# Lower experts' rows gathered and added on POOL during the last MoE blocks, and the last block's y added by a slot matrix on PE

## The chip, the cores and the metric

One core of one Trainium2 chip runs the whole program. The metric is the device time of one execution in microseconds (us), the median of three runs. Names of engines: PE (TensorE), DVE (VectorE), ACT (ScalarE), POOL (GpSimd), SP (SyncE, which issues loads).

## The reference, cut to what matters

A token mixer (not touched by the change) gives `x` for 544 tokens (512 of a prompt, 32 samples) of width 1024. Then:

```python
def grouped_moe(x, w_router, router_bias, w_gate, w_up, w_down):
    xt = x.reshape(B * T, D)
    probs = jax.nn.softmax(xt @ w_router + router_bias, axis=-1)      # 16 experts in 4 groups of 4
    grp_score = lax.top_k(grp, TOP_K)[0].sum(-1)
    g_idx = lax.top_k(grp_score, 1)[1][:, 0]                          # one group for each token
    top_w, top_i = lax.top_k(jnp.where(emask, probs, -1.0), TOP_K)    # two experts inside it
    top_w = top_w / jnp.sum(top_w, axis=-1, keepdims=True)
    for e in range(N_EXPERTS):
        h = jax.nn.silu(xt @ w_gate[e]) * (xt @ w_up[e])
        y = y + gates[:, e:e + 1] * (h @ w_down[e])

x = layer_norm(ALPHA * x + grouped_moe(x, ...), ln2_g, ln2_b)
```

All is f32. A token has two experts, both in one group of four consecutive experts.

## The kernel before, in words

The tokens are five tiles (four of 128 rows, one of 32). After the mixer and the first layer norm, x1 stands in `xr` and in DRAM by token (`x1_by_token`). DVE computes the routing and a slot for each of the 2 x 544 choices: expert e owns the 128 slots of block e, and up to eight overflow blocks take what doesn't fit (their count, `n_over`, is read at the end; with these inputs it is 0). `slot_f` and `slot_i` hold ten columns, five tiles for the first choice and five for the second, `gw` their gates.

Then 16 blocks follow, one expert each, in the order of their numbers. Each engine has its own written order, `step(bi, par)`, with semaphores between them. For block b:

* SP (`moe_loads`, L505 on) loads six chunks of weights of 1 MB each (gate in two, up in two, and down of block b-1 in two) into a ring of eight `raw` places, as soon as DVE has used the chunk eight before.
* ACT (`mhi`, L859) rounds a chunk to f32r, DVE (`mlo`, L1322) subtracts to get the low part: a 128x2048 tensor_tensor whose two inputs are both in SBUF. PE makes three products (hi hi, hi lo, lo hi) of each piece: `gate_up` (L1777) and `down` (L1789). There are three places for split chunks.
* POOL gathers the x1 rows of the next block by `ids` (`gather`, L629), and stores the y of two blocks before from `ysb[par]` to `y_by_slot` in DRAM (`store`, L646). y leaves PSUM in two halves, one by ACT (L882), one by DVE (`y_half`, L1339).
* PE transposes x (`x_turn`, L1767) and h (`h_turn`, L1799); ACT and DVE copy them to hi and lo (L864, L869, L1327, L1332). `hidden` (L1347) multiplies silu(gate) and up on DVE.

After block 15, POOL waits for both stores, reads the overflow count (L661), and issues ten indirect gathers (L672), two for each tile, into `y_a` and `y_b`, which lie where `raw` was. DVE makes eleven diagonal matrices (`diag`, L1411 and L1415): ALPHA, and the gates of each tile and choice. PE's `weigh` (L1865) forms, for each tile and each half of 512 columns, ALPHA x + g1 y_a + g2 y_b in PSUM, as three f32 products with a diagonal as weights; those with x for tiles 0 to 3 come before the gathers have landed. The fifth tile uses the banks of the first, so it waits for DVE to have read them (`s_fg`). Then DVE takes mean and variance (L1425, L1428), subtracts and scales (L1431), ACT takes the root (L945) and scales the tile (L949), POOL adds the bias (L677), SP stores. For the last tile DVE does scale and bias itself (L1438).

In front of block 0, DVE does `first_lo` for three chunks, then `overflow_table` (L1302 to L1308, 22 small linked operations), then `x_lo(0, 0)`, for which PE's first product waits. At the very start of the program POOL fills the overflow blocks of `y_by_slot` with zeros (L574), 8 blocks in one DMA.

## Time and profile before

| what | value |
|---|---|
| three runs | 698.58, 697.02, 699.57 us; median 698.58 |
| the run that was profiled | 699.09 us, its span 697.3 us |
| PE busy | 663.2 us (95%), 3847 instructions |
| DVE busy | 505.2 us (72%) |
| ACT busy | 344.4 us (49%) |
| POOL busy | 134.8 us (19%) |
| granted TensorE clock, mean | 0.976 |

The span is the time from the first to the last event of the profile; the run's own time is 1.8 us longer. The profile names a group of instructions by line, engine, operation, and `written tile<-read tiles`, and puts idle time before an instruction down to what ended it. Matmul records are pipelined, and an f32 product of 512 columns shows as two records.

### The profile page before, as it was taken

The page shows a single profiled execution, that of the slowest core. Times are in us where ns is not written, and L with a number is a line of the kernel's source. Part 1 is how long each engine was busy: PE and PEld are TensorE (multiplying, and loading weights), DVE is VectorE, ACT ScalarE, POOL GpSimd, SP SyncE. Part 2 cuts the span into 40 slices and gives each one's busy share as a digit, 9 for nine tenths or more (in the row PEclk, how much of TensorE's full clock was granted, in tenths as well). Part 3 has the DMA queues.
Part 4 walks back from the last instruction along what each step waited for, and adds up shares of the span by engine and source line. Part 5 has one row for each costly group of instructions (what it writes and reads, how often), then busy time and mean ns, then how long its engine had stood idle before and what let it go on. Part 6 is the DMA issues. An engine that isn't in the chain of part 4 may idle for free. (4 is left out here: it accounts for less than half of the span.)

```text
span 697.3 us, 9659 instructions
## 1 busy us (share of the span) xinstructions
PE 663.2 (95%) x3847; PEld 559.2 (80%) x3847; DVE 505.2 (72%) x579; ACT 344.4 (49%) x339; POOL 134.8 (19%) x81
## 2 busy tenths in 40 slices
PE   6999999988999999999979999999999999999786
PEld 5999899988997897577857888888888888888531
DVE  4226336798766384758684999999999999999626
ACT  4537412222226141111505777777777777777402
POOL 0001414422131220400020011111111111100055
PEclk9999999999999999999898999999999999999998
DMA  8951111211612105069346999999999999994164
GB/s 285 381 198 62 61 61 62 69 53 61 190 53 85 53 16 193 0 185 410 138 160 274 328 417 419 397 415 409 407 415 411 404 413 406 410 404 173 47 242 158
DMA packets 48689, 162.56 MB, mean 233 GB/s; under 512 B 4294, under 2 KB 23450, under 8 KB 36364
## 3 DMA queue, kind: packets, MB, share of 16 engines
q1 hardware_dynamic: 41756, 136.62, 51.4%
q0 software_dynamic: 6896, 25.43, 9.3%
q8 instruction: 25, 0.41, 0.2%
q14 instruction: 12, 0.10, 0.0%
HBM read 142.61 MB, written 19.44 MB: 232 GB/s over the span
## 5 line engine op out<-in xcount | busy, mean ns | idle before, releaser
L1322 DVE TENSOR_TENSOR RA<-FA,RA 128x2048 fp32r<-128x2048 f32 x93 | 212.9, 2290 | 29.4 <-ACT RA L859 28.7
L859 ACT ACTIVATE RA<-FA 128x2048 fp32r<-128x2048 f32 x93 | 178.9, 1924 | 46.3 <-PE bank L1777 30.6
L1777 PE MATMUL bank<-RA 128*128 128x512 f32 x768 | 186.9, 399 | 2.7 <-DVE RA L1327 2.6
L1777 PEld LDWEIGHTS bank<-RA 128*128 128x128 f32 x768 | 142.9, 191 | 34.6 <-DVE RA L1327 3.5
L1504 PE MATMUL bank<-RA 128*128 128x272 f32 x432 | 110.3, 292 | 0.0
L1505 PE MATMUL bank<-RA 128*128 128x272 f32 x432 | 109.6, 290 | 0.0
L1789 PE MATMUL bank<-RA 128*128 128x512 f32 x384 | 89.9, 390 | 1.4 <-DVE RA L1332 1.4
L1789 PEld LDWEIGHTS bank<-RA 128*128 128x128 f32 x384 | 72.0, 188 | 16.5 <-DVE RA L1332 1.6
L1504 PEld LDWEIGHTS bank<-RA 128*128 128x128 f32 x432 | 82.5, 191 | 0.0
L1505 PEld LDWEIGHTS bank<-RA 128*128 128x128 f32 x432 | 82.3, 191 | 0.0
L983 DVE TENSOR_TENSOR RA<-FA,RA 128x2048 fp32r<-128x2048 f32 (+1 forms) x18 | 48.6, 2700 | 27.3 <-ACT RA L713 27.0
L713 ACT ACTIVATE RA<-FA 128x2048 fp32r<-128x2048 f32 (+1 forms) x18 | 33.6, 1867 | 58.1 <-PE bank L1505 27.5
L1497 PE MATMUL bank<-RA 128*128 128x256 f32 (+1 forms) x480 | 58.8, 282 | 2.0 <-ACT FA L725 2.0
L1497 PEld LDWEIGHTS bank<-RA 128*128 128x128 f32 (+1 forms) x480 | 56.1, 172 | 4.7 <-ACT FA L725 2.4
L629 POOL DMA_INDIRECT FA<-x_by_token,ids x16 | 39.7, 2483 | 79.8 <-DVE ids L1299 60.2
L646 POOL DMA_DIRECT2D y_by_slot<-FA x16 | 9.1, 571 | 236.5 <-DVE FA L1339 236.5
L1659 PE MATMUL bank<-RA 128*128 128x512 f32 x192 | 48.3, 408 | 0.0
L1659 PEld LDWEIGHTS bank<-RA 128*128 128x128 f32 x192 | 36.7, 194 | 10.9 <-issue 2.5
L584 POOL TENSOR_TENSOR FA<-FA 128x1024 f32<-128x1024 f32 (+1 forms) x7 | 16.6, 2365 | 113.5 <-PE bank L1539 69.3
L760 ACT ACTIVATE FA<-FA 128x2048 f32<-128x2048 f32 (+1 forms) x7 | 13.6, 1947 | 49.7 <-POOL FA L585 49.7
L1042 DVE COPY_PREDICATED FA<-masks,bank 128x512 f32<-128x512 uint8 x28 | 20.1, 734 | 22.3 <-PE bank L1539 21.9
L1539 PE MATMUL bank<-FA 128*128 128x128 f32 x256 | 31.0, 278 | 3.9 <-DVE FA L1042 3.9
(237 smaller groups left out, 774.1 us busy)
## 6 DMA issues: line engine op xcount, KB each, us to landing
FA<-w_up SPq DMA_DIRECT2D x32, 1024.0 KB, 7.6
FA<-w_gate SPq DMA_DIRECT2D x32, 1024.0 KB, 7.3
FA<-w_down SPq DMA_DIRECT2D x32, 1024.0 KB, 7.8
FA<-w_in SPq DMA_DIRECT2D x13, 1024.0 KB, 4.9
y_by_slot<-FA POOLq DMA_DIRECT2D x16, 512.0 KB, 7.5
y_by_slot<-FA POOLq DMA_DIRECT2D x1, 4096.0 KB, 18.1
FA<-w_out SPq DMA_DIRECT2D x4, 1024.0 KB, 5.0
FA<-x_prompt SPq DMA_DIRECT2D x8, 256.0 KB, 5.4
```

The lines of the kernel that those rows point to most:

```text
L629: pool.indirect_dma_start(out=xg[par], out_offset=None, in_=x1_dram, in_offset=bass.IndirectOffsetOnAxis(ap=ids[:, bi:bi + 1].bitcast(U32) ...
L713: nc.scalar.activation(split[o % 2][0][:, cs], raw[o % 3][:, cs], ACT.Copy).then_inc(s_hi, 1)
L859: nc.scalar.activation(split[split_slot(bi, j)][0], raw[place], ACT.Copy).then_inc(m_hi, 1)
L983: tt_(split[o % 2][1][:, cs], raw[o % 3][:, cs], f(split[o % 2][0][:, cs]), ALU.subtract).then_inc(s_lo, 1)
L1322: tt_(sl[1], raw[place], f(sl[0]), ALU.subtract).then_inc(m_lo, 1)
L1497: last = mm(pb[0:rows, 0:CW], xT[x_][:, kt, tok(j)], w_[:, kt, :], start=(kt == 0 and i == 0), stop=(kt == KT - 1 and i == 2))
L1504: mm(pb[:, 0:HT], lhs, xT[x_][:, kt, 0:HT], start=first, stop=end)
L1505: last = mm(ps[:, 0:HT], lhs, xT[x_][:, kt, HT:T], start=first, stop=end)
L1539: last = mm(bank[4 + p % 3][:, cols], lf[:, h, cols], rf[:, h, cols], start=True, stop=True)
L1659: last = mm(w_bank(half, tt)[0:rows, :], xT[x_][:, k0 + kt, tok(tt)], w_[:, kt, :], start=(conv and kt == 0 and i == 0), stop=(not conv an ...
L1777: last = mm(out[:, :], xgT[par][x_][:, kt, :], w[w_][:, t, :], start=(kt == 0 and i == 0), stop=(kt == KT - 1 and i == 2))
L1789: last = mm(bank[5 + g][:, :], hT[x_][:, kt, :], w[w_][:, t, 512 * g:512 * g + 512], start=(kt == 0 and i == 0), stop=(kt == 3 and i == 2))
```

## The change

The new kernel is cut here to what it does in the MoE part.

* The blocks go through the experts in another order, `expert_at(s) = 4 * (s % 4) + s // 4`: first the first expert of each group, last the fourth of each. A token's two experts lie in one group, so the one with the earlier block ("lower") is always in block 11 or before. The tables of slots follow this order (`SM_POS`, `SM_LEFT`).
* DVE sorts each token's two slots and gates into lower and higher (`order_slots`, 15 small linked operations and five of 128x128). The gates are divided by ALPHA, and the last layer norm works on x + y/ALPHA with its epsilon divided by ALPHA squared. `order_slots` also writes `g_tok`: for each token its slot within the last block, as a row with the gate at that place. PE transposes these five tiles after the steps of blocks 0 and 1 and ACT copies them to `g_last`.
* `overflow_table` moves behind `x_lo(0, 0)` on DVE, with `order_slots` behind it, both ahead of DVE's step 0.
* POOL, between its steps of blocks 14 and 15, gathers the lower rows of tiles 0 and 1, multiplies each by its gate and adds x (two instructions a tile). After the store of block 13 it does so for tiles 2 to 4. SP stores block 14, after all five lower gathers have landed. Then POOL gathers the higher rows, without block 15, which is never stored: its slots in `y_by_slot` hold zeros, since the fill at the start now covers 11 blocks.
* The scaled sums of tiles 0 and 1 are completed by DVE (one instruction each), those of tiles 2 to 4 by ACT (scale) and POOL (add).
* PE forms each tile's sum in PSUM by `g_last` times `ysb[1]`, block 15's y in SBUF, and the identity times the completed sum: four products a tile. The eleven diagonals are gone.

The diff, cut to its core:

```diff
+def expert_at(s, i=0):
+    return 4 * (s % 4) + s // 4 + i
...
-                    load(count_of(s, j) - 1, source(j, bi, bi - 1))
+                    load(count_of(s, j) - 1, source(j, expert_at(s, i), expert_at(s - 1, i)))
...
+            for tt in range(NTT):
+                sp.wait_ge(s_ga[tt][0], 16)
+            sp.wait_ge(m_ya, E - 1)
+            sp.wait_ge(m_yd, E - 1)
+            sp.dma_start(yg_dram.rearrange("(b p) n -> b p n", p=P)[E - 2], ysb[0]).then_inc(s_st14, 16)
...
+            def add_first(tt, again):
+                pool.wait_ge(s_ga[tt][0], 32 if again else 16)
+                rows = rows_of(tt)
+                nc.gpsimd.tensor_scalar(y_of(tt, 0), y_of(tt, 0), gs_lo[0:rows, tt:tt + 1], None, ALU.mult).then_inc(s_scaled, 1)
+                pool.wait_ge(s_scaled, (NTT if again else 0) + tt + 1)
+                nc.gpsimd.tensor_tensor(y_of(tt, 0), y_of(tt, 0), xr[0:rows, tt, :], ALU.add).then_inc(s_xa, 1)
...
-            for bi in range(2, E):
+            for bi in range(2, E - 1):
                 step(bi, bi % 2)
-            store(E - 2, 0)
-            store(E - 1, 1)
-            for par in range(2):
-                pool.wait_ge(m_st[par], 16 * (E // 2))
+            pool.wait_ge(s_sort, 1)
+            pool.wait_ge(m_st[0], 16 * (E // 2 - 1))
+            pool.wait_ge(m_st[1], 16 * (E // 2 - 2))
+            for tt in range(2):
+                gather_rows(tt, 0)
+            for tt in range(2):
+                add_first(tt, False)
+            step(E - 1, 1)
+            pool.wait_ge(m_st[1], 16 * (E // 2 - 1))
+            for tt in range(2, NTT):
+                pool.wait_ge(m_lo, 6 * E - NRAW + tt // 2)
+                gather_rows(tt, 0)
+            for tt in range(2, NTT):
+                add_first(tt, False)
+            pool.wait_ge(s_st14, 16)
+            pool.wait_ge(m_lo, 6 * E - NRAW + 5)
+            for tt in range(NTT):
+                gather_rows(tt, 1)
...
+            for tt in range(2, NTT):
+                pool.wait_ge(s_bs, tt - 1)
+                pool.wait_ge(s_xa, tt + 1)
+                nc.gpsimd.tensor_tensor(y_of(tt, 1), y_of(tt, 1), y_of(tt, 0), ALU.add).then_inc(s_xbp, 1)
...
             first_lo(2)
+            x_lo(0, 0)
             overflow_table()
-            x_lo(0, 0)
+            order_slots()
             step(0, 0)
...
-            ts_(diag[:, 0, :], ident, ALPHA, None, ALU.mult).then_inc(s_diag, 1)
...
+            for tt in range(2):
+                dve.wait_ge(s_ga[tt][1], 16)
+                dve.wait_ge(s_xa, tt + 1)
+                stt(y_of(tt, 1), y_of(tt, 1), gs_hi[:, tt:tt + 1], y_of(tt, 0), ALU.mult, ALU.add).then_inc(s_xbd, 1)
...
-                for n, y in enumerate((y_a, y_b)):
-                    pe.wait_ge(s_ga[tt][n], 16)
-                    last = weigh(tt, 1 + 2 * tt + n, y, False, n == 1)
+                for g, i in enumerate(sum_banks(tt)):
+                    mm(bank[i][0:rows, :], g_last[:, tok(tt)], ysb[1][:, 512 * g:512 * g + 512], start=True, stop=False)
+                if tt < 2:
+                    pe.wait_ge(s_xbd, tt + 1)
+                else:
+                    pe.wait_ge(s_xbp, tt - 1)
+                for g, i in enumerate(sum_banks(tt)):
+                    last = mm(bank[i][0:rows, :], ident[0:rows, 0:rows], y_of(tt, 1)[:, 512 * g:512 * g + 512],
+                              start=False, stop=True)
```

Where the instructions stand on POOL, the engine on which most of it turns. Before, from the last gather of x (L629) to the end of the blocks: stores of blocks 12, 13, and then 14 and 15 (L646), and the read of the overflow count (L661).

```order
L629 DMA FA<-x_by_token,ids 128x1024 [waits moe_x_transposed]
L646 DMA y_by_slot<-FA 128x1024 [waits moe_y_dve,moe_y_act]
L646 DMA y_by_slot<-FA 128x1024 [waits moe_y_dve,moe_y_act,moe_x_transposed]
L646 DMA y_by_slot<-FA 128x1024 [waits moe_y_dve,moe_y_act] x2
L661 TENSOR_LOAD itab [waits slots,moe_y_stored1,moe_y_stored0]
```

After, from the same gather of x (L665) and the store of block 12 (L682) to the gathers of tiles 2 to 4:

```order
L665 DMA FA<-x_by_token,ids 128x1024 [waits moe_x_transposed]
L682 DMA y_by_slot<-FA 128x1024 [waits moe_y_dve,moe_y_act]
L693 DMA FA<-y_by_slot,slot_i 128x1024 [waits moe_y_stored1,moe_y_stored0,slots_in_order]
L693 DMA FA<-y_by_slot,slot_i 128x1024
L701 TENSOR_SCALAR FA<-FA 128x1024 [waits rows_gathered0_0]
L703 TENSOR_TENSOR FA<-FA 128x1024 [waits term_scaled_by_pool]
L701 TENSOR_SCALAR FA<-FA 128x1024 [waits rows_gathered1_0]
L703 TENSOR_TENSOR FA<-FA 128x1024 [waits term_scaled_by_pool]
L682 DMA y_by_slot<-FA 128x1024 [waits moe_y_dve,moe_y_act,moe_x_transposed]
L693 DMA FA<-y_by_slot,slot_i 128x1024 [waits moe_lo,moe_y_stored1]
L693 DMA FA<-y_by_slot,slot_i 128x1024 [waits moe_lo]
L693 DMA FA<-y_by_slot,slot_i 32x1024 [waits moe_lo]
```

Two gathers and four instructions of arithmetic have come between the stores of blocks 12 and 13.

POOL after that, up to the overflow count: the three tiles' arithmetic stands ahead of the higher rows' gathers.

```order
L701 TENSOR_SCALAR FA<-FA 128x1024 [waits rows_gathered2_0]
L703 TENSOR_TENSOR FA<-FA 128x1024 [waits term_scaled_by_pool]
L701 TENSOR_SCALAR FA<-FA 128x1024 [waits rows_gathered3_0]
L703 TENSOR_TENSOR FA<-FA 128x1024 [waits term_scaled_by_pool]
L701 TENSOR_SCALAR FA<-FA 32x1024 [waits rows_gathered4_0]
L703 TENSOR_TENSOR FA<-FA 32x1024 [waits term_scaled_by_pool]
L693 DMA FA<-y_by_slot,slot_i 128x1024 [waits moe_lo,moe_y_of_block_14_stored]
L693 DMA FA<-y_by_slot,slot_i 128x1024 x3
L693 DMA FA<-y_by_slot,slot_i 32x1024
L726 TENSOR_LOAD itab [waits slots]
```

Before, all ten gathers stood behind the overflow count; now two stand ahead of the first four instructions of arithmetic, three between the two pieces of it and five behind, all ahead of the count.

## Rows read from the trace of the kernel before

**Rows 1.** The chain that ended last, its main pieces: start us, us, what.

```profile
661.16 3.55 issue
...
666.40 4.29 DMA FA<-y_by_slot,slot_i
...
672.81 17.56 PE bank L1865 x40
...
693.62 1.27 DVE FA L1438
```

**Rows 2.** Timeline of the tail: start us, us, engine, line, operation, tiles, [idle before].

```profile
653.63 5.73 PE L1789 MATMUL bank<-RA 128*128 128x512 f32 x24 [1.41 <-DVE RA L1332]
...
688.42 1.15 ACT L949 ACTIVATE FA<-FA 128x1024 f32<-128x1024 f32 x1 [1.42 <-DVE FA L1436]
...
689.64 2.34 POOL L677 TENSOR_TENSOR FA<-FA 128x1024 f32<-128x1024 f32 x1 [1.08 <-ACT FA L949]
```

**Rows 3.** Page, groups: busy us, mean ns of one, idle before and what ended it.

```profile
L1322 DVE TENSOR_TENSOR RA<-FA,RA 128x2048 fp32r<-128x2048 f32 x93 | 212.9, 2290 | 29.4 <-ACT RA L859 28.7
...
L1777 PE MATMUL bank<-RA 128*128 128x512 f32 x768 | 186.9, 399 | 2.7 <-DVE RA L1327 2.6
```

**Rows 4.** Timeline of POOL: the stores of blocks 12 and 13.

```profile
614.90 0.58 POOL L646 DMA_DIRECT2D y_by_slot<-FA  x1 [14.26 <-DVE FA L1339]
632.85 0.56 POOL L646 DMA_DIRECT2D y_by_slot<-FA  x1 [17.37 <-DVE FA L1339]
```

**Rows 5.** Timeline of POOL: a memset of 1024 elements a partition.

```profile
264.78 0.96 POOL L621 MEMSET FA<- 128x1024 f32 x1 [16.18 <-PE bank L1634]
```

**Rows 6.** Timeline of 133 to 141 us: POOL and DVE together.

```profile
133.47 2.05 POOL L584 TENSOR_TENSOR FA<-FA 128x1024 f32<-128x1024 f32 x1 [9.56 <-PE bank L1539]
...
134.21 3.46 DVE L983 TENSOR_TENSOR RA<-FA,RA 128x2048 fp32r<-128x2048 f32 x1
...
135.48 3.94 POOL L585 TENSOR_TENSOR FA<-FA 128x1024 f32<-128x1024 f32 x1
```

**Rows 7.** Timeline of POOL: gathers in front of the blocks, inside and behind.

```profile
365.37 0.94 POOL L629 DMA_INDIRECT FA<-x_by_token,ids  x1 [4.73 <-PE bank L1767]
...
597.84 2.80 POOL L629 DMA_INDIRECT FA<-x_by_token,ids  x1 [0.30 <-issue]
...
666.40 0.98 POOL L672 DMA_INDIRECT FA<-y_by_slot,slot_i  x1 [5.23 <-issue]
```

**Rows 8.** DMA issues at 597.8, 614.9, 650.7 and 666.4; last number: us to landing.

```profile
FA<-x_by_token,ids POOLq DMA_INDIRECT x1, 10.8
...
y_by_slot<-FA POOLq DMA_DIRECT2D x1, 512.0 KB, 7.1
...
y_by_slot<-FA POOLq DMA_DIRECT2D x1, 512.0 KB, 2.9
...
FA<-y_by_slot,slot_i POOLq DMA_INDIRECT x1, 4.3
```

**Rows 9.** Stretches: length, busy us (x) PE, PEld, DVE, ACT, POOL; granted clock.

```profile
366.00:367.00 1.00, 0.00 (x0) 0.00 (x0) 0.96 (x3) 0.22 (x1) 0.30 (x1) 0.63 1.04 430
...
373.00:374.00 1.00, 1.00 (x6) 0.82 (x5) 0.00 (x0) 0.74 (x1) 0.00 (x0) 0.96 0.32 131
...
668.00:671.00 3.00, 0.55 (x2) 0.20 (x2) 0.00 (x0) 0.00 (x0) 2.39 (x3) 1.00 0.89 259
```

**Rows 10.** Timeline in front of block 0 and of block 1.

```profile
361.94 0.17 DVE L1302 TENSOR_TENSOR FA<-FA 128x16 f32<-128x16 f32 x1
...
365.13 1.08 ACT L864 ACTIVATE RA<-bank 128x512 fp32r<-128x512 f32 x2 [17.34 <-PE bank L1767]
...
366.33 1.29 DVE L1327 TENSOR_TENSOR RA<-bank,RA 128x512 fp32r<-128x512 f32 x2
...
375.21 2.29 DVE L1322 TENSOR_TENSOR RA<-FA,RA 128x2048 fp32r<-128x2048 f32 x1 [7.59 <-ACT RA L859]
...
382.47 1.70 PEld L1777 LDWEIGHTS bank<-RA 128*128 128x128 f32 x8 [0.51 <-DVE RA L1327]
```

More of the change, by code:

```diff
@@ L101, in constants @@
     s[:, SM_BLK:SM_BLK + NBLK + 1] = P * np.arange(NBLK + 1)
+    for pos in range(E):
+        s[:, SM_POS + expert_at(pos)] = P * pos
+        s[:, SM_LEFT + expert_at(pos)] = E - pos
     s[:, SM_TOK:SM_TOK + NTT] = np.arange(NTT)[None, :] * P + p[:, None]
@@ L677, in _ @@
                 nc.gpsimd.tensor_tensor(xr[:, tt, :], xr[:, tt, :], ln[:, 3, :], ALU.add).then_inc(s_yp, 1)
-            for par in range(2):
-                pool.wait_ge(m_st[par], 16 * (E // 2))
         @block.scalar
@@ L937, in _ @@
                             act.wait_ge(m_use, 6 * E + 6 * v + 6)
[L938 to L939 removed]
+                            act.wait_ge(s_st14, 16)
+                            act.wait_ge(m_st[0], 16 * (E // 2 - 1 + r) + 16 * RING * i)
+                            nc.scalar.activation(ysb[0][:, 0:512], bank[5][:, :], ACT.Copy).then_inc(m_ya, 1)
+                for tt in range(2, NTT):
+                    act.wait_ge(s_ga[tt][1], 32)
             nc.scalar.activation(shift[:, 0:1], eps_ln, ACT.Sqrt)
+            for tt in range(2, NTT):
+                act.wait_ge(s_ga[tt][1], 16)
+                nc.scalar.activation(y_of(tt, 1), y_of(tt, 1), ACT.Copy, scale=gs_hi[0:rows_of(tt), tt:tt + 1]).then_inc(s_bs, 1)
             for tt in range(NTT):
@@ L1273, in _ @@
             tt_(t3(base), in_tile.rearrange("p (t e) -> p t e", t=NTT),
-                small[:, SM_BLK:SM_BLK + E].unsqueeze(1).broadcast_to([P, NTT, E]), ALU.add)
-            link(stt(tmp, before, -1.0, eo, ALU.add, ALU.add))
+                small[:, SM_POS:SM_POS + E].unsqueeze(1).broadcast_to([P, NTT, E]), ALU.add)
+            link(stt(tmp, before, -1.0, small[:, SM_LEFT:SM_LEFT + E], ALU.add, ALU.add))
             link(stt(t3(over), in_tile.rearrange("p (t e) -> p t e", t=NTT), float(P),
@@ L1824, in step, with turn_gates @@
                 gate_up(bank[3], par, split_slot(bi, 5), 1, count_of(bi, 5))
+            def turn_gates(tiles):
+                for tt in tiles:
+                    rows, c0 = P if tt < 4 else NS, (tt % 4) * P
+                    last = tr(bank[7][:, c0:c0 + rows], g_tok[0:rows, tt, :], ident[0:rows, 0:rows])
+                last.then_inc(s_gtt, 1)
             keep_clock(28)
@@ L1828, in _ @@
             step(0, 0)
+            pe.wait_ge(s_sort, 2)
+            turn_gates(range(4))
             step(1, 1)
+            pe.wait_ge(s_gc, 1)
+            turn_gates((4,))
             step(2, 0)
```

142 lines of the change are left out of this document (90 added, 52 removed).

## The prediction

> **What bounds the kernel now.** I read the chain of waits first, since it says what ends last [rows 1]. The last block's y is stored, the store lands, POOL reads the overflow count and issues the gathers; the first gather takes 4.29 us, and then TensorE (PE) weighs for 17.56 us without a wait worth naming. The part named "issue" (3.55 us) is that store in flight. After PE's last product at 690.37 (672.81 + 17.56) there follow about 4.5 us of layer norm on VectorE (DVE), to 694.89, and the last store. So of the 36 us behind the last expert's products, some 10 are store and gather and 20 are PE's weighing. The timeline of the tail [rows 2] gives PE's price: an f32 product of 512 columns is two records, 17.56 / 40 = 0.439 us each, so 0.88 us a product. Of 30 such products, 8 ran while the gathers were in flight and 22 stand on the chain.
>
> The blocks before the tail are the second thing to read [rows 3]: in 768 records of gate and up products PE idles 2.7 us, so PE sets their pace. DVE works 2.29 us on each of six chunks per block, 13.7 us of the 17.95 between two blocks' stores (632.85 - 614.90 [rows 4]), with copies and products besides, and idles 0.3 us before a chunk (29.4 / 93). It is nearly full, with some 2 us to spare per block.
>
> **The change, part by part.**
>
> *Work on PE in the tail.* Of 30 products, 20 stay: a tile takes two with the last block's y in place and two with the identity over a sum made elsewhere. Ten products less are 8.8 us. The first two (G0) need only ysb, so they run at once; the other 18 wait for the first tile's sum. From that sum to PE's end: 36 records x 0.439 = 15.8 us.
>
> *Who makes the sums.* POOL, for all five tiles, multiplies and adds the lower expert's rows (10 instructions), and adds the scaled higher rows of tiles 2 to 4. A plain POOL tensor_tensor of 128x1024 takes 2.34 us [rows 2]. The multiply with one tensor input is in no row. Its ends are the memset, 0.96 us, which reads nothing [rows 5], and the tensor_tensor, 2.34, which reads twice. I take 1.2, nearer to the memset, because one read and one write can go side by side. The page "GPSIMD Engine Reference" of the Trainium skill, section 3.1, has 1.03 cycles an element for such bodies, about 0.9 us here; with 1.0 instead of 1.2 the sum below would be 1.0 us smaller. No run shows it yet.
>
> *What these cost DVE and POOL.* When POOL works from SBUF beside a DVE tensor_tensor with two SBUF inputs, they exclude each other [rows 6]. DVE's L983, the same form as the block's chunk work at L1322 (128x2048, 2.29 alone), takes 3.46 because it starts 0.7 us into POOL's 2.05, and POOL's next one takes 3.94, about twice its 2 us, because it waits for DVE's to end. They alternate. The new multiplies and adds of tiles 0 and 1 fall into the last two blocks, where DVE works such chunks one after another.
>
> *The chain of POOL, by the clock of the trace before.* (1) Block 12's store is issued at 614.90 and lands 7.1 later [rows 4, 8]: 622.0. (2) The gather of tile 0: the gathers of x at that load take 10.8 from issue to landing [rows 8]: 632.8. The end below is 6.1 (4.3 for an unloaded gather [rows 8], plus 1.86 of generation [rows 7]); I take the loaded row since weights still load until about 637. (3) POOL's four instructions with three DVE chunks let in between: 2 x (1.2 + 2.34) + 3 x 2.29 = 13.95: 646.8. Only now comes the store of block 13, issued at 632.85 before [rows 4]: 14 us late. (4) It lands 2.9 later, as the store at 650.7 did [rows 8]: 649.7. (5) The gather of tile 2: 2.80 to generate beside DVE [rows 7] and 3.3 more (4.3 less the 0.98 of generating [rows 7]), 655.8. (6) Tiles 2 to 4: 3 x 3.54 = 10.6, and one DVE chunk (the last down chunk) between, 2.29: 668.7. (7) Only then does POOL issue the higher rows' gathers: 4.3 to the first landing, 673.0. SP's store of block 14 waits for all low gathers (about 658) and lands by 662, so it isn't late. (8) DVE scales and adds 128x1024, taken as the 1.27 of L1438, which has as many elements a partition [rows 1]: 674.3. (9) PE, 15.8: 690.1. Tiles 2 to 4 go over ACT (1.15 [rows 2]) and POOL (2.34) and are about 1 us ahead of PE each; nothing added.
>
> *Generation beside DVE, row against rule.* The gather's own time on POOL is 0.94 us when DVE does small work and 2.80 in the blocks [rows 7]. The Trainium skill, page "SBUF — State Buffer", section "SBUF: two separate sides", names as what starves descriptor generation a DVE operation in a 2-port mode; the page "VectorE: DVE Perf Modes" says that tensor_tensor cannot run in one. By that rule the two gathers in steps 2 and 5 would each generate in 0.94 beside the chunk work, 3.7 us sooner together, and the sum would end 3.7 lower. The row speaks against it, and I use the row.
>
> *PE's clock.* Between G0's end (about 667) and 674.3 PE has nothing to do, 7 us. In front of block 0 it waits for x until DVE has its low part at 367.6 [rows 10], and the granted clock falls to half within 366 to 367 (0.63 is its mean there; 1.2 of 2.4 GHz) and is back at 373, where the mean is 0.96 [rows 9]. From 367.6 to 373.1 PE works at half speed, so 2.7 us are lost. Between 668 and 671 it is busy only 0.55 of 3 us and keeps its clock [rows 9]. These are the ends, 0 and 2.7; the gap of 7 us is nearer to the case with the fall (no product for 2.6 us), but some of the low stretch may pass before work begins, so I take 2.2: 692.3.
>
> *The blocks on PE.* DVE loses to POOL's first four instructions about 7.1 us, less what its slack and the two chunks of lead give, so PE ends block 15 some 4 to 5 us late (664 instead of 659.4 [rows 2]). That costs nothing: G0 still ends before 674.3. It is the cover that goes first if POOL's chain were shorter.
>
> *The front.* DVE now turns x first and makes the tables after. It did the table's 22 small operations from 361.94 to 366.33, while ACT's first half of x, begun at 365.13, was ready at 365.7, so PE starts up to 0.6 sooner; 15 more linked operations (0.2 each) and five 128x128 ones make 4.1 us, and with the 4.4 of the table they fill the idle of 7.59 before L1322 at 375.21, ending at about 375.5 [rows 10]. That chunk is then 0.3 late with more than 1 us in hand. Four transposes (0.5) fill PE's wait of 0.51 at 382.47 [rows 10]. Net -0.2, ends -0.6 and +0.6. The larger fill (11 blocks for 8) ends long before its waiter, the load of the states: nothing. The order of experts only changes addresses: nothing.
>
> **Sum.** PE ends at 692.3 instead of 690.37: +1.9; the layer norm behind it is the same 4.5; front -0.2. So **+1.7 us**: a span of 699.0 and, with the 1.8 us around it, 700.8 for the run profiled (699.09 before). That run stands 0.5 above the median of 698.58, so the forecast for the median is 698.58 + 1.7 = **700.3 us**. The ten products saved go into POOL's queue.
>
> **The rivals.**
>
> A, *low rows sooner*. The first gather meets less traffic than the x gather does (block 12's store has landed by then), taking 8 instead of 10.8, and PE's clock holds. 2.8 less and 2.2 less, of which a chunk of DVE (2.29) at a worse moment can take back half: -2.2 to -3.3, 695.3 to 696.4. By the rule on generation above, 3.7 less alone: 696.6. For it: rows 8 differ by more than 6 us between loaded and not. Chance 0.17.
>
> B, *no exclusion*. POOL's instructions run beside DVE's: 3 chunks (6.9), one more (2.3) and the late block fall away, PE idles 3 us at most and keeps its clock (2.2). 1.7 - 11.4 = -9.7, 688.9; if generation then took 0.94 in steps 2 and 5 too, 685.2. Against it stand five places like rows 6. Chance 0.10.
>
> C, *the multiply as dear as a tensor_tensor* (the other sign). Place: POOL between the low gathers and the higher ones, five multiplies on the chain. Each 0.1 us above 1.2 adds 0.5. At 2.34 they add 5.7: +7.4, 706.0. It decides from 1.56 upward (+3.5). For it: POOL's operations all show about 1 us for each 1024-element stream. Against: the memset row. Chance 0.18.
>
> D, *POOL in the tail*: the three adds and the four last adds on POOL (7 x 2.34 = 16.4) begin at about 677 and end at 693.5, beside a last DVE operation with two SBUF inputs, which would wait up to 2.3: +4.0, 702.6. Chance 0.07.
>
> **How the numbers follow.** A measurement here can tell about 0.5%, 3.5 us. The forecast has 0.48 (within 3.5 us: 0.35, slower 0.10, faster 0.03). A 0.17 (faster 0.08, same 0.09); B 0.10 faster; C 0.18 (slower 0.16, same 0.02); D 0.07 slower in 0.05, same 0.02. Together faster 0.21, same 0.48, slower 0.31. The range runs from 693, below A and short of B, to 707, above C: outside are B and the ends of C and A, under 2 in 10. The forecast's own range is 697 to 704.
>
> **What would show each step.** Right: block 13's store issued near 647; DVE's chunks in block 15 at 3.3 to 4.6 us beside POOL; the last down products ending at 663 to 665; POOL's ten low instructions ending near 669; a gap of 6 to 8 us on PE after the first two tail products, then the clock at 0.5; 20 f32 products, PE's end near 692. Wrong: chunks at 2.29 throughout (B); a multiply at or under 1.0 or above 1.6 (A, C); PE's gap under 3 us, which would put its end under 685.

## The result, and the profile after

The changed kernel takes 704.36 us (median of 4, 702.87 to 707.49) beside 699.08 us for the kernel before on the same chip: ratio 1.0084, 95% interval 1.0061 to 1.0108, slower by 5.3 us. The forecast was 700.3 in a range of 693 to 707; the time is in the range, but the sign given the best chance was "same" (0.48), "slower" had 0.31, and the forecast difference, +1.7 us, lies below the measured interval (+4.3 to +7.5). The profiled execution was the slowest of the four (707.49 us, span 705.6), so a second one was taken later; both are used below.

The page of the first profile, its share of engines, the chain that ended last by line, and a group:

```profile
PE 659.0 (93%) x3832; PEld 557.9 (79%) x3832; DVE 513.4 (73%) x591; ACT 348.9 (49%) x344; POOL 177.6 (25%) x92
...
POOL FA L701 3%; DMA FA<-y_by_slot,slot_i 2%; PE bank L1993 2%; POOL FA L703 1%; PE bank L1987 1%; POOL FA L693 1%; DMA y_by_slot<-FA 1%; DVE FA L1538 0%; DVE FA L1532 0%; DVE FA L1523 0%; DVE FA L1545 0%; DVE FA L1535 0%; DVE FA L1543 0%; POOLq L726 0%; POOLq L681 0%
...
L1426 DVE TENSOR_TENSOR RA<-FA,RA 128x2048 fp32r<-128x2048 f32 x93 | 217.4, 2342 | 19.5 <-ACT RA L931 19.0
```

PE works 4.2 us less than before (663.2), POOL 43 us more (134.8). Of the lines in the chain that ended last the largest is now POOL's multiply, L701, where before it was PE's weighing [rows 1]. DVE's chunk has gone from 2290 to 2342 ns on the mean of 93 [rows 3].

POOL's timeline, first profile, answers [rows 4]: start us, us, engine, line, operation, tiles.

```profile
614.24 0.58 POOL L682 DMA_DIRECT2D y_by_slot<-FA  x1 [14.28 <-DVE FA L1443]
...
632.74 4.96 POOL L701 TENSOR_SCALAR FA<-FA 128x1024 f32<-128x1024 f32 x1 [6.32 <-DMA FA<-y_by_slot,slot_i]
637.79 2.59 POOL L703 TENSOR_TENSOR FA<-FA 128x1024 f32<-128x1024 f32 x1
640.37 7.00 POOL L701 TENSOR_SCALAR FA<-FA 128x1024 f32<-128x1024 f32 x1
...
649.99 0.63 POOL L682 DMA_DIRECT2D y_by_slot<-FA  x1
```

The end of its chain of waits: start us, us, what.

```profile
658.64 2.87 POOL FA L701
...
663.98 2.83 POOL FA L701
...
669.22 2.81 POOL FA L701
...
672.11 2.33 POOL FA L703
674.44 0.16 POOLq L726
674.60 4.25 DMA FA<-y_by_slot,slot_i
...
678.88 1.29 DVE FA L1523
...
680.21 3.78 PE bank L1993 x4
...
696.53 1.84 PE bank L1993 x4
```

A multiply alone on POOL takes 2.83 to 2.87 us, above the 1.2 of the sum and above both its ends. The higher rows' gathers leave behind the tenth low instruction (674.44), and PE's identity products start at 680.21 and end at 698.37.

The second profile is of the same kernel, an execution of 701.13 us, the fastest of its five (median 703.31), so the two profiles stand at the two ends. POOL's timeline in it:

```profile
611.28 0.57 POOL L682 DMA_DIRECT2D y_by_slot<-FA  x1 [14.30 <-DVE FA L1443]
...
628.18 2.86 POOL L701 TENSOR_SCALAR FA<-FA 128x1024 f32<-128x1024 f32 x1 [4.71 <-DMA FA<-y_by_slot,slot_i]
631.12 3.17 POOL L703 TENSOR_TENSOR FA<-FA 128x1024 f32<-128x1024 f32 x1
634.28 4.88 POOL L701 TENSOR_SCALAR FA<-FA 128x1024 f32<-128x1024 f32 x1
639.25 2.59 POOL L703 TENSOR_TENSOR FA<-FA 128x1024 f32<-128x1024 f32 x1
641.78 0.63 POOL L682 DMA_DIRECT2D y_by_slot<-FA  x1
...
650.57 2.85 POOL L701 TENSOR_SCALAR FA<-FA 128x1024 f32<-128x1024 f32 x1 [0.18 <-DMA FA<-y_by_slot,slot_i]
653.50 3.62 POOL L703 TENSOR_TENSOR FA<-FA 128x1024 f32<-128x1024 f32 x1
...
667.75 1.01 POOL L693 DMA_INDIRECT FA<-y_by_slot,slot_i  x1 [0.16 <-issue]
```

PE in its tail, same execution:

```profile
652.72 5.74 PE L1896 MATMUL bank<-RA 128*128 128x512 f32 x24 [1.41 <-DVE RA L1436]
660.05 1.96 PE L1987 MATMUL bank<-FA 128*128 128x512 f32 x4 [1.59 <-DVE FA L1443]
673.43 3.78 PE L1993 MATMUL bank<-FA 128*128 128x512 f32 x4 [11.43 <-DVE FA L1523]
```

Executions issue the store of block 12 at 611.06 to 614.90 us, up to 3.8 us apart, so traces are compared from that store on. In the first profile block 13's store follows it by 35.8 us, in the second by 30.5; in four runs below with the same order up to there (2 to 5) it is 30.5 to 30.8. In the first profile POOL was held by DVE's chunks more often than is usual.

### The profile page after: what moved, and what is told of

Read it like the earlier page. It is cut to its first block and busy times, and to the rows that moved or that the text cites. A ratio compares the mean times of both kernels' runs of the same rounds, so it can differ in the third digit from the quotient of the medians.

```text
span 705.6 us, 9662 instructions
## 1 busy us (share of the span) xinstructions
PE 659.0 (93%) x3832; PEld 557.9 (79%) x3832; DVE 513.4 (73%) x591; ACT 348.9 (49%) x344; POOL 177.6 (25%) x92
## 5 line engine op out<-in xcount | busy, mean ns | idle before, releaser
L1426 DVE TENSOR_TENSOR RA<-FA,RA 128x2048 fp32r<-128x2048 f32 x93 | 217.4, 2342 | 19.5 <-ACT RA L931 19.0
L1611 PE MATMUL bank<-RA 128*128 128x272 f32 x432 | 109.1, 290 | 0.0
L1612 PE MATMUL bank<-RA 128*128 128x272 f32 x432 | 108.5, 288 | 0.0
L665 POOL DMA_INDIRECT FA<-x_by_token,ids x16 | 39.5, 2466 | 76.8 <-DVE ids L1384 60.0
L682 POOL DMA_DIRECT2D y_by_slot<-FA x14 | 8.2, 583 | 194.4 <-DVE FA L1443 194.4
L832 ACT ACTIVATE FA<-FA 128x2048 f32<-128x2048 f32 (+1 forms) x7 | 13.6, 1949 | 49.4 <-POOL FA L621 49.4
L1646 PE MATMUL bank<-FA 128*128 128x128 f32 x256 | 30.7, 277 | 3.9 <-DVE FA L1126 3.9
```

The costliest lines, as they stand in the source:

```text
L665: pool.indirect_dma_start(out=xg[par], out_offset=None, in_=x1_dram, in_offset=bass.IndirectOffsetOnAxis(ap=ids[:, bi:bi + 1].bitcast(U32) ...
L1426: tt_(sl[1], raw[place], f(sl[0]), ALU.subtract).then_inc(m_lo, 1)
L1611: mm(pb[:, 0:HT], lhs, xT[x_][:, kt, 0:HT], start=first, stop=end)
L1612: last = mm(ps[:, 0:HT], lhs, xT[x_][:, kt, HT:T], start=first, stop=end)
L1646: last = mm(bank[4 + p % 3][:, cols], lf[:, h, cols], rf[:, h, cols], start=True, stop=True)
```

## The experiments

In all of them "from block 12's store" is counted from the issue of that store on POOL, and "end of the last down products" is that of block 15.

**1. No multiplies.** POOL's five low multiplies are left out, so the low rows go into the sum without their gates.

```diff
-                nc.gpsimd.tensor_scalar(y_of(tt, 0), y_of(tt, 0), gs_lo[0:rows, tt:tt + 1], None, ALU.mult).then_inc(s_scaled, 1)
-                pool.wait_ge(s_scaled, (NTT if again else 0) + tt + 1)
```

> The changed kernel without POOL's five multiplies of the lower rows (the gates of the lower experts are left out, so the first term is unweighted). Theory 1, POOL's chain sets PE's first sum and a multiply costs 2.83 us in it: block 13's store is issued near 641 instead of 650, the higher rows' gathers near 660 instead of 674.6, PE's first identity product near 666 instead of 680.2 and PE keeps its clock; about 16 us less than the changed kernel's 704.4, so 688, a ratio of 0.985 to the kernel before. Theory 2, the exclusion with DVE and the late block 15 set the end, with the adds alone enough for it: block 15 ends as late as before (663.8) and the time stays at 701 or above.

Measured: 695.24 us, ratio 0.9938 (0.9913 to 0.9962), faster than both kernels, but not 688. Store 13 went out 24.6 from block 12's store. What held the rest back, in the timeline of DVE and POOL:

```profile
649.02 7.22 DVE L1424 TENSOR_TENSOR RA<-FA,RA 128x2048 fp32r<-128x2048 f32 x1 [0.43 <-ACT RA L929]
...
654.03 4.40 POOL L701 TENSOR_TENSOR FA<-FA 32x1024 f32<-32x1024 f32 x1
...
656.16 0.68 DVE L1441 COPY FA<-bank 128x512 f32<-128x512 f32 x1
...
659.86 0.97 POOL L693 DMA_INDIRECT FA<-y_by_slot,slot_i  x1 [1.42 <-DMA y_by_slot<-FA]
```

POOL's three adds stand at 649.35 to 658.44, back to back, and DVE's one chunk of 2.29 us takes 7.22 beside them: it is listed 0.33 us ahead of the first, while POOL still generates a gather (to 649.33), but is let in only behind the second add, at about 654, and the third add is held for it (4.40 instead of 2.34). Block 15's y, block 14's store and PE's last down products (to 668.6 instead of 663.8) are late in its wake, and the first identity product (671.26) follows PE's own late work without a gap. Without the multiplies the kernel is 9 us faster; the next bound is adds against chunks.

**2. Higher gathers ahead of tiles 3 and 4.** Only the order of POOL's instructions changes.

```diff
-            for tt in range(2, NTT):
-                add_first(tt, False)
+            add_first(2, False)
...
             for tt in range(NTT):
                 gather_rows(tt, 1)
+            for tt in range(3, NTT):
+                add_first(tt, False)
```

> Only the order on POOL: the higher rows' gathers stand ahead of the arithmetic of tiles 3 and 4 (behind that of tile 2). Nothing is left out. Theory 1, what counts is what stands ahead of these gathers: they start near 664 instead of 674.6, the first identity product near 669.5; but POOL then works the two tiles (10.4 us) and three adds (7.0) and four last adds (9.4) one after the other, so of the 10.6 us some 5 arrive: 699.5, a ratio near 1.000. Theory 3, the sum of POOL's work sets the end, whatever its order: unchanged, 704.

Measured: 699.49 us, ratio 1.0013 (0.9989 to 1.0038). PE of this run:

```profile
666.35 1.98 PE L1994 MATMUL bank<-FA 128*128 128x512 f32 x4 [0.23 <-DVE FA L1524]
...
671.60 1.88 PE L1988 MATMUL bank<-FA 128*128 128x512 f32 x4
679.96 2.93 PE L1994 MATMUL bank<-FA 128*128 128x512 f32 x3 [6.48 <-POOL FA L749]
```

The first identity product comes at 666.35, but PE then waits 6.48 us for tile 2's sum, since POOL still has tiles 3 and 4 to do. POOL's queue is as long; the wait has only moved behind two tiles.

**3. Clock kept.** Fifty f32r products into an unused bank keep PE busy in its gap.

```diff
+                if tt == 0:
+                    idle = RA[:, 0:640]
+                    for _ in range(50):
+                        mm(bank[2][:, :], idle[:, 512:640], idle[:, 0:512], start=True, stop=True)
```

> The changed kernel with 50 products of f32r (about 0.22 us each, 11 us) into an unused bank behind the first two tail products, into the gap of 13.6 us in which PE has nothing. If the half clock costs what the trace shows (18.16 us for 40 records where 15.8 were due), PE's end comes 2.3 us sooner: 702.1. If the slow first products wait for something else, nothing changes: 704.4. If the 50 products end after the first sum is there, it is later, at most by 2 us.

Measured: 702.22 us, ratio 1.0055 (1.0026 to 1.0084), against 1.0084 without them; the intervals overlap. In the trace the clock stays at 1.00 and PE takes 15.8 us from its first identity product to its end, 18.2 and 18.6 in the two profiles of the change. So the clock's part of the sum, 2.2, is borne out by the trace (2.3 to 2.7); that the whole time falls by it, 2.1 us by the medians, is not clear of the noise.

**4. Multiply by a constant.** The gates of the low rows are replaced by 0.5.

```diff
-gs_lo[0:rows, tt:tt + 1], None, ALU.mult)
+0.5, None, ALU.mult)
```

> The changed kernel with POOL's multiply by the constant 0.5 instead of a gate per partition (the gates of the lower experts are left out). It measures the disputed price. If the 2.83 us lie in the operand per partition, the instruction takes 1.0 to 1.5 us alone and the chain is shorter by 5 x 1.5 = 7 us; if it is the price of the operation itself on POOL, 2.8 us and the same time as the changed kernel, 704.

Measured: one run, 702.42 us. The multiplies that nothing holds take 2.76 to 2.80 us. The gate as an operand is worth 0.07; the price is the instruction's.

**5. The multiply in other forms.** Tile 2's has two inputs, tile 3's is cut in halves of 512.

```diff
+                elif tt == 2:
+                    nc.gpsimd.tensor_tensor(y_of(tt, 0), y_of(tt, 0), gs_lo[0:rows, tt:tt + 1].broadcast_to([rows, D]), ALU.mult).then_inc(s_scaled, 1)
...
+                    for g in range(2):
+                        part = y_of(tt, 0)[:, 512 * g:512 * g + 512]
+                        nc.gpsimd.tensor_scalar(part, part, gs_lo[0:rows, tt:tt + 1], None, ALU.mult).then_inc(s_scaled, 1)
```

> The changed kernel with the low multiplies of tiles 2 and 3 in other forms: tile 2's as an instruction with two inputs (the gate spread over the row by stride 0), tile 3's as two instructions of 512 elements; tile 4's as it was. All stand behind block 13's store with no chunk of VectorE's beside them. T1 (the instruction with a scalar has a dearer rate for each element than the one with two inputs): tile 2's takes 2.3 to 2.4 us against 2.8 of tile 4's, and tile 3's halves 1.4 to 1.5 us each. T2 (a fixed price of over 1 us for each instruction with a scalar): halves over 1.8 us each. T3 (any multiply with the gate is dear): tile 2's takes 2.8 us or more.

POOL's timeline in this run, with DVE's chunk and, once more by itself, the second of the two halves:

```profile
653.48 1.89 POOL L705 TENSOR_TENSOR FA<-FA 128x1024 f32<-128x1024 f32 x1
...
655.59 4.38 DVE L1435 TENSOR_TENSOR RA<-FA,RA 128x2048 fp32r<-128x2048 f32 x1
...
657.80 5.16 POOL L710 TENSOR_SCALAR FA<-FA 128x512 f32<-128x512 f32 x2
661.40 1.56 POOL L710 TENSOR_SCALAR FA<-FA 128x512 f32<-128x512 f32 x1
...
665.36 2.83 POOL L702 TENSOR_SCALAR FA<-FA 32x1024 f32<-32x1024 f32 x1
```

Two inputs: 1.89. The two halves have to be read apart, since a chunk did stand beside the first, against what was expected: that chunk had waited for the add ahead of it and ran until 659.97, so the half issued at 657.80 took 3.61, and the second, with nothing beside it, 1.56. Their mean, 2.58, is the price of neither. By the second, the instruction with a scalar costs about 0.3 us fixed (2 x 1.56 - 2.83) and 2.5 for its 1024 elements, an estimate from one half. That is T1, a dearer rate, although the form with two inputs was cheaper still than T1 had it; a fixed price of over 1 us (T2) is ruled out. What tile 2 won went into the held half, and the time is the changed kernel's (one run, 704.51).

**6. All five multiplies with two inputs**, in their places; nothing is left out.

```diff
-                nc.gpsimd.tensor_scalar(y_of(tt, 0), y_of(tt, 0), gs_lo[0:rows, tt:tt + 1], None, ALU.mult).then_inc(s_scaled, 1)
+                nc.gpsimd.tensor_tensor(y_of(tt, 0), y_of(tt, 0), gs_lo[0:rows, tt:tt + 1].broadcast_to([rows, D]), ALU.mult).then_inc(s_scaled, 1)
```

> The changed kernel with one word of it other: the five low multiplies stay on GpSimd, in their places, but as an instruction with two inputs, the gate spread over the row by stride 0. In the run with other forms tile 2's took 1.89 us so, against 2.83 of the instruction with a scalar. Nothing is left out. T1 (the size of this one instruction set the sign): each multiply 1.9 us where no chunk stands beside it, block 13's store near 648, tiles 2 to 4 end 2.9 us sooner than there, all ten end near 669.5 instead of 674.4, first identity product near 675.3, time 698.5 to 700.5, ratio to before 0.999 to 1.003, no longer clearly slower. T2 (two inputs shut VectorE's chunks out of block 15 longer, and the store of block 14 with them): block 15's last down products end past 666, higher gathers at 672 or later, time 702 to 705.

Measured: 703.92 us, ratio 1.0075 (1.0047 to 1.0104). My expected 698.5 to 700.5 was wrong; the time is T2's, but its signs are not there (last down products to 664.8, higher gathers at 670.26). POOL's timeline, with one chunk of DVE, says why:

```profile
614.25 0.58 POOL L682 DMA_DIRECT2D y_by_slot<-FA  x1 [14.26 <-DVE FA L1443]
...
632.02 1.89 POOL L701 TENSOR_TENSOR FA<-FA 128x1024 f32<-128x1024 f32 x1 [5.60 <-DMA FA<-y_by_slot,slot_i]
632.70 3.36 DVE L1426 TENSOR_TENSOR RA<-FA,RA 128x2048 fp32r<-128x2048 f32 x1
633.99 4.31 POOL L703 TENSOR_TENSOR FA<-FA 128x1024 f32<-128x1024 f32 x1
638.26 3.94 POOL L701 TENSOR_TENSOR FA<-FA 128x1024 f32<-128x1024 f32 x1
642.28 4.32 POOL L703 TENSOR_TENSOR FA<-FA 128x1024 f32<-128x1024 f32 x1
646.55 0.61 POOL L682 DMA_DIRECT2D y_by_slot<-FA  x1
...
659.47 3.94 POOL L701 TENSOR_TENSOR FA<-FA 128x1024 f32<-128x1024 f32 x1
```

The multiply is 0.94 us cheaper alone, but now, from the second on, the instructions beside chunks are held for one (4.31, 3.94, 4.32, and again 3.94 at 659.47). Block 13's store is at 32.3 from block 12's, 1.8 later than in the second profile. Of that, 0.9 is the row of tile 0, which landed later; the four instructions took 14.5 us, where they took 12.8 to 13.8 with the dearer form (second profile, runs 2 to 5). Behind that store the three tiles win 2.1 (655.15 to 670.11, against 650.57 to 667.59), so the higher gathers leave at 56.0 instead of 56.5.

A chunk in the second profile shows the difference between the forms; it starts 1.58 us into the multiply of 628.18:

```profile
629.76 2.28 DVE L1426 TENSOR_TENSOR RA<-FA,RA 128x2048 fp32r<-128x2048 f32 x1
```

Neither is held. Chunks that start 0.6 to 0.8 us into a multiply with a scalar take 2.50 to 2.61 (runs 2, 4 and 5), so that form lets a chunk in about 0.9 to 1.0 us after its start, though it takes 2.83. Above, the chunk of 632.70 starts 0.68 into the multiply with two inputs and takes 3.36: it is let in 1.75 into the 1.89. The other way round the dear form is held too: the second multiply of the second profile, at 634.28, starts while a chunk runs and takes 4.88. So the cheaper form keeps the chunks out longer, which pushes them into POOL's next instruction. That is the reading of a few rows. What the run shows by its time is that expectation T1 was wrong as a cause: the price of one form alone didn't set the sign.

**7. Arithmetic of tiles 0 and 1 behind block 13's store.**

```diff
-            for tt in range(2):
-                add_first(tt, False)
             step(E - 1, 1)
...
-            for tt in range(2, NTT):
+            for tt in range(NTT):
                 add_first(tt, False)
```

> The changed kernel with the arithmetic of low tiles 0 and 1 moved on GpSimd behind block 13's store and the gathers of tiles 2 to 4, so that all ten instructions stand together. T1 (GpSimd's work is a sum: 5 x 2.84 + 5 x 2.34 = 25.9 us, 3 to 5 us more for being shut out by chunks, behind gathers that now start near 635): store of block 13 near 632, arithmetic from 640 to 668 to 671, higher gathers there, time 698 to 701. T2 (the order makes no difference, or store 14 and block 15 become late behind the adds, as in the run without multiplies): last down products end past 666 and the higher gathers leave at 674 or later, time 703 to 706.

Measured: 706.65 us, ratio 1.0127 (1.0100 to 1.0155), the time of T2 but not its mechanism: the last down products end at 661.7. POOL of this run:

```profile
631.63 0.57 POOL L682 DMA_DIRECT2D y_by_slot<-FA  x1 [5.74 <-DVE FA L1441]
639.43 2.02 POOL L693 DMA_INDIRECT FA<-y_by_slot,slot_i  x1 [7.23 <-DMA y_by_slot<-FA]
...
673.38 1.01 POOL L693 DMA_INDIRECT FA<-y_by_slot,slot_i  x1 [0.16 <-issue]
```

The store goes out early, as expected, but now while the weights of the last block (and the two gathers) are under way, and it lands 7.5 us after its issue, as the store of block 12 did before with weights alone beside it (7.1 [rows 8]); in the changed kernel it is 3.0. POOL waits idle meanwhile. In the changed kernel POOL's arithmetic lies over that traffic.

**8. Low multiplies on ACT, adds on POOL**; nothing is left out.

```diff
+            def scale_low(tt):
+                act.wait_ge(s_ga[tt][0], 16)
+                nc.scalar.activation(y_of(tt, 0), y_of(tt, 0), ACT.Copy, scale=gs_lo[0:rows_of(tt), tt:tt + 1]).then_inc(s_as, 1)
```

> The changed kernel with the five low multiplies on ScalarE (two in its step of block 15, three behind its roundings of the hidden half), and GpSimd left with the adds. Nothing is left out of the computation. GpSimd's work is that of the run without multiplies (695.24 us), so T1 (only the time of the multiplies on GpSimd counted) expects 694 to 697, with the store of block 13 issued near 640 and block 15's last down products ending late, near 668, because the adds and VectorE's chunks shut each other out. T2 (ScalarE's scales, put ahead of its copies and roundings of the last block, delay block 15 further): last down products past 671, time 698 to 702.

Measured: 697.25 us, ratio 0.9973 (0.9960 to 0.9987), just above T1's range and below T2's. An ACT scale takes 1.14 us. Store 13 came at 30.7 from block 12's, as late as in the changed kernel, because the first add waited for ACT; but the last down products end at 660.7, not late, so that part of the expectation was wrong. Here the last chunk (654.83, 2.28) had started ahead of the adds and was not held; in run 1 it was not let in ahead of them. PE had 5.81 us without work ahead of its first identity product and took 17.9 us from there to its end, at first at the low clock (0.50 granted from 668 to 672); run 1, with no gap there, took 15.8. That is why run 8 is behind run 1 although its first identity product is sooner.

**9. Tiles 0 to 2 on DVE, 3 and 4 on ACT and POOL behind the higher gathers.**

```diff
             for tt in range(2):
-                add_first(tt, False)
+                pool.wait_ge(s_ga[tt][0], 16)
...
+            def low_by_dve(tt):
+                dve.wait_ge(s_ga[tt][0], 16)
+                stt(y_of(tt, 0), y_of(tt, 0), gs_lo[:, tt:tt + 1], xr[:, tt, :], ALU.mult, ALU.add).then_inc(s_xad, 1)
```

> The changed kernel, with its low rows' arithmetic shared out anew: tiles 0 to 2 get x + gate * row from VectorE in one instruction each (one behind the last block's hidden half, two behind its last chunk), tiles 3 and 4 are scaled on ScalarE and added on GpSimd behind the higher gathers. GpSimd only waits for the first two low gathers ahead of block 13's store and goes to the higher gathers as soon as block 14's store has landed. T1 (the arithmetic on GpSimd sets the end, 30 us of it ahead of the higher gathers): store of block 13 issued near 634 instead of 650, last low gather by 645, store of block 14 near 651, higher gathers near 654 to 656, first identity product 662 to 666, TensorE's end 678 to 682, time 685 to 689, ratio to before near 0.983. T2 (landings set it): the higher gathers leave as early but land late, and the identity products start after 670, time above 694. T3 (the three VectorE instructions make block 15 late as the adds on GpSimd did): its last down products end past 666, time 692 to 695.

Measured: 693.55 us, ratio 0.9918 (0.9897 to 0.9939), faster than before but short of T1. The higher gathers left even sooner than expected (651.44), and the first identity product came within the expected time (663.73). Then, on POOL and DVE:

```profile
658.36 11.53 DVE L1544 SCALAR_TENSOR_TENSOR FA<-FA 128x1024 f32<-128x1024 f32 x2
...
658.55 5.66 POOL L702 TENSOR_TENSOR FA<-FA 128x1024 f32<-128x1024 f32 x2
664.17 7.92 POOL L759 TENSOR_TENSOR FA<-FA 128x1024 f32<-128x1024 f32 x3
```

Two DVE sums of 1.28 us each take 11.53 beside five POOL adds; the second is let in only behind the fourth of them. PE waits 2.62 us for tile 1, and the granted clock is 0.57 in 670 to 674.

**10. All low tiles on DVE; POOL's adds wait for DVE's two sums.** The cut below is against the kernel of run 9.

```diff
-            for tt in (3, 4):
-                add_x(tt)
...
+            low_by_dve(3)
+            low_by_dve(4)
...
+                pool.wait_ge(s_xbd, 2)
                 nc.gpsimd.tensor_tensor(y_of(tt, 1), y_of(tt, 1), y_of(tt, 0), ALU.add).then_inc(s_xbp, 1)
```

> The run with tiles 0 to 2 on VectorE, taken on: all five low tiles get x + gate * row from VectorE (tiles 3 and 4 behind its copy of the last y), ScalarE and GpSimd do none of it, and GpSimd's three adds of the higher rows wait until VectorE's two sums of tiles 0 and 1 are done. In the run before this, VectorE's two sums took 11.53 us at 658.36 beside five GpSimd adds back to back (2.56 us without them), and TensorE waited 2.62 us for tile 1 and ran at half clock after it. T1 (the two engines' two-input instructions shut each other out there): the two sums take 2.5 us, TensorE's ten pairs of products run without a gap from 660 to near 679, time 687 to 690, ratio to before near 0.985. T2 (the sums were late for the higher rows' landings instead): the sums end no sooner, TensorE still waits at tile 1, time 692.5 to 694.5 as in the run before this.

Measured: 689.16 us, ratio 0.9871 (0.9854 to 0.9889), the best of all: 9 us faster than before, 15 faster than the change. DVE and POOL of this run:

```profile
660.54 2.46 DVE L1493 SCALAR_TENSOR_TENSOR FA<-FA 128x1024 f32<-128x1024 f32 x2
662.93 2.46 DVE L1533 SCALAR_TENSOR_TENSOR FA<-FA 128x1024 f32<-128x1024 f32 x2
...
665.58 6.97 POOL L748 TENSOR_TENSOR FA<-FA 128x1024 f32<-128x1024 f32 x3 [6.37 <-DVE FA L1533]
```

Four DVE instructions in 4.85 us, three POOL adds in 6.97, neither held. The run changes two things at once, two adds fewer on POOL and the wait; what each is worth alone is not shown. DVE does with 1.28 us a tile, in gaps it had, what POOL did in 5.2. PE runs from 664.25 to 680.2 without a gap, with a granted clock of 1.00 in all stretches from 658 to 674.

**11. The front alone.** Before, with only the two `x_lo` differences ahead of the overflow table.

```diff
-            overflow_table()
             x_lo(0, 0)
+            overflow_table()
```

> The kernel before with only one part of the change: block 0's two x differences are put ahead of the overflow table on VectorE. T1 (the front gives 0.2 to 0.7 us, as store 12 was issued 0.66 us earlier in the changed kernel): time 0.2 to 0.7 us under before, ratio 0.9990 to 0.9997, which five rounds may not tell from one; in the trace TensorE starts block 0's products near 367.8 and step 1's near 381.5 instead of 382.5. T2 (the 0.66 us in the changed kernel came from the order computation's other lines, not from this move): step 1's start stays at 382.4.

Measured: 698.49 us, ratio 0.9988 (0.9972 to 1.0004). It gains 0.8 us by the medians, which can't be told from nothing. The granted clock in 367 to 370 was 1.00 in this run and 0.50 before; it was kept in the first profile of the change too, but in the second the same 24 records took 7.37 us instead of 5.75. PE's wait ahead of them was 2.01 us in all three (2.58 before), so with the same wait the clock fell in one execution and not in two.

**12. The change once more.**

> The changed kernel as it is, profiled a second time, because its first profiled execution (707.49 us) was its slowest of four: there the first two multiplies took 4.96 and 7.00 us and block 13's store went out at 649.99, whereas three other kernels with the same instructions up to there show 2.8, 4.8 and 644.1 to 645.3. T1 (that execution was shut out by chunks more often than is usual): a profiled execution near 703 to 705 us has the store of block 13 near 645, the low rows' arithmetic done near 670 to 671, the first identity product near 676 and TensorE's end near 694.5 to 695.5, so that of the 4 us over the forecast most come from the three multiplies behind that store. T2 (this kernel always loses it there): the store again near 650, and the executions differ elsewhere. Median again 703.5 to 705.5 and ratio 1.006 to 1.010 in both.

Measured: 703.31 us (median of 5), ratio 1.0083 (1.0044 to 1.0121); the execution that was profiled, 701.13, lies below the 703 to 705 that T1 asked for. T1, counted from block 12's store (this execution was 3.0 us ahead there): store 13 at 30.5, higher gathers at 56.5 (60.4 in the first profile).

The runs in one table, from block 12's store in us, in the order of their ratio (4 and 5 are single runs and have none):

| kernel | store 13 | higher gathers | first identity product | PE's end | ratio to before |
|---|---|---|---|---|---|
| low rows all on DVE (10) | 22.5 | 38.3 | 50.4 | 66.4 | 0.9871 |
| tiles 0 to 2 on DVE (9) | 23.6 | 38.2 | 50.5 | 71.0 | 0.9918 |
| no multiplies (1) | 24.6 | 46.1 | 57.5 | 73.3 | 0.9938 |
| multiplies on ACT (8) | 30.7 | 50.9 | 56.6 | 74.5 | 0.9973 |
| before | 18.0 | | | 75.5 | 1 |
| higher gathers sooner (2) | 30.7 | 46.2 | 51.8 | 76.0 | 1.0013 |
| clock kept (3) | 30.5 | 56.5 | 62.8 | 78.6 | 1.0055 |
| multiplies with two inputs (6) | 32.3 | 56.0 | 61.7 | 80.6 | 1.0075 |
| the change, second profile | 30.5 | 56.5 | 62.2 | 80.7 | 1.0083 |
| the change, first profile | 35.8 | 60.4 | 66.0 | 84.1 | 1.0084 |
| arithmetic behind store 13 (7) | 17.9 | 59.7 | 65.3 | 83.3 | 1.0127 |

PE's end follows the ratio in every row but that of the first profile, the slowest execution of its kernel. The higher gathers carry most of it: sooner gathers go with a sooner end, but for run 2, where PE waits later for POOL. Runs 9 and 10 issue them together and differ by the DVE sums; run 3 differs from the change by the clock.

## Why the prediction came out as it did

By the prediction's own steps, in us from block 12's store (the forecast's clock less 614.90):

| step ends | forecast | second profile | first profile |
|---|---|---|---|
| 2, row of tile 0 landed | 17.9 | 16.9 | 18.5 |
| 3, store of block 13 | 31.9 | 30.5 | 35.8 |
| 4, it has landed | 34.8 | 33.5 | 38.7 |
| 5, row of tile 2 | 40.9 | 39.3 | 44.4 |
| 6, ten instructions done | 53.8 | 56.3 | 60.2 |
| 7, higher row of tile 0 | 58.1 | 60.8 | 64.6 |
| 8, first sum | 59.4 | 62.2 | 66.0 |
| 9, PE's end, with the clock | 77.4 | 80.7 | 84.1 |

*The chain* was right: every step stands in that order, and PE's gap, which I put at 7 us, only grew (11.43 and 13.60).

*Step 6, tiles 2 to 4 on POOL, was mis-sized.* It was 3 x (1.2 + 2.34) and one chunk, 12.9; it measured 17.0: three multiplies at 2.84 add 4.9, and the chunk's shut-out was worth 1.3 (an add of 3.62) instead of 2.29. That is 4.1 us too little, more than the whole 3.3 by which PE's end in the second profile is over the forecast; sooner landings (1.3) and the clock (0.5 more) make most of the rest. PE's end stands 80.7 from block 12's store instead of 75.5 before: +5.2, where +1.9 was forecast; the medians have +5.3 and +4.3.

*The range of the multiply's price was wrong too.* Its ends were the memset, 0.96 [rows 5], and the add, 2.34 [rows 2], as if one input could cost no more than two. It measured 2.83, about 2.5 of it for its 1024 elements (run 5), and the same product with two inputs 1.89. The Trainium skill, page "GPSIMD Engine Reference", section 3.1, has a rate of 1.03 cycles an element, about 0.9 us; the measurement decides, and speaks against both it and my 1.2.

*Step 3 was right for the wrong reason.* The 13.95 held two multiplies at 1.2 and three chunks at 2.29. In the second profile it was 13.6: multiplies of 2.86 and 4.88, the adds 3.17 and 2.59. Two multiplies dearer by 3.3 us together were made up by waits of 3.2 in place of the 6.9 for three whole chunks: the two errors cancel, which is luck. Run 6 shows the other side.

*Rival C* ("the multiply as dear as a tensor_tensor") is the case that came. Its condition, over 1.56, was met well, yet the time is below its 706.0, since what it adds in step 3 was covered. Its rule, 0.5 us for each 0.1, gives 708.5 at the measured 2.83, where the change takes 704.36, and 703.8 at 1.89, where run 6 takes 703.92: 0.94 us less for each multiply should have brought 4.7 us and brought 0.4. So the price of that one instruction is not the cause by itself. What the runs show is that the five tiles' ten instructions on POOL, with the shut-outs between them and DVE's chunks, stand ahead of the higher gathers; take them off POOL and the time falls by 15 us (10).

*Rivals A, B, D.* A: tile 0's row landed 16.9 after block 12's store in the second profile, 1.0 sooner than forecast, and 18.5 in the first; the clock fell. B: no; single chunks took 3.89 and 4.50 beside POOL in the two profiles, and 7.22 in run 1. D: DVE's last operation took 1.27 us; nothing was held at the very end.

*Generation beside DVE*: 1.4 to 2.0 us for the first two gathers in the two profiles (2.3 to 2.6 in run 9), 2.8 for one in the first. The rule of the Trainium skill weighed in the prediction ("SBUF — State Buffer", section "SBUF: two separate sides") would have 0.94 there; the rows have more, but mostly less than my 2.80. The three gathers behind block 13's store in the first profile show the two cases side by side: 1.01 and 0.95 (653.24, 654.56) with no chunk running, 2.78 (655.81) beside the chunk of 655.57.

*Block 15*: the last down products were forecast 4 to 5 us late and harmless. From block 12's store they ended at 44.5 before, 49.5 in the first profile and 47.2 in the second, so 5.0 and 2.7 late, harmless in both. In run 1, with a shorter chain, that lateness became the bound, as the sentence on the cover said.

*The clock*: 2.2 was taken; from the first identity product to PE's end it was 18.2 and 18.6 against 15.8 with the clock kept (3): 2.3 to 2.7.

*The front*: -0.2 was taken. What the runs show is -0.8 for the move of `x_lo` alone, within its noise; for the whole front nothing was measured by itself.

## What to carry to other kernels

Products saved on PE bring nothing if what feeds the rest of them gets longer: before moving work to an idle engine, count what stands in its queue ahead of the DMA that the tail waits for. Work that needs SBUF beside a nearly full DVE goes best to DVE itself, as one instruction of 1.28 us in its gaps, or to ACT (1.14 for a scale); and two-input instructions of DVE and POOL that would meet can be put one behind the other by a wait, as in the best run here, though not shown by itself. An unseen instruction's price isn't bounded by another that reads more: here the form with one input cost 2.83, that with two 1.89. And a mean over two instructions can be the price of neither: 2.58 was one of 1.56 and one that was held.

## What the runs showed of the hardware

* POOL's tensor_scalar of f32 in SBUF: 2.83 us for 1024 elements a partition, at 128 and at 32 partitions, 2.76 with a constant, 1.56 for 512 elements (one instruction). The same product with the gate as a broadcast second input: 1.89; an add: 2.34.
* Two-input instructions of POOL and DVE, both from SBUF, hold each other, and back-to-back instructions of POOL can pass a waiting one of DVE: a DVE chunk of 2.29 took 7.22, let in behind the second of three adds, and two DVE sums of 2.5 took 11.53 beside five.
* POOL's multiply with a scalar is held when a DVE chunk is running at its start (4.88). It holds a chunk only for about its first 0.9 to 1.0 us of 2.83: chunks that start 0.6 to 0.8 into it took 2.50 to 2.61, those that start 1.58 (second profile) and 1.77 into it (run 3) took 2.28. This is read from these five chunks.
* A store of 512 KB lands 3.0 us after its issue when it is alone, 7.1 with weights under way, 7.5 with weights and two gathers.
